# The opening of a three-block transformer kernel: shift and scale of the first norm in another order

## What is computed

```python
mod = cond @ w_mod[l] + b_mod[l]            # cond = silu(c), one row of 1024
sh1, sc1, g1, ... = jnp.split(mod, 9, axis=-1)
h = rms_norm(x, norm_g[l, 0]) * (1.0 + sc1) + sh1
x = x + 0.5 * g1 * swiglu(h, w_ffn1_gu[l], w_ffn1_down[l])
```

## Time and profile before

| | us |
|---|---|
| median of 3 runs | 1767.01 (1766.74 to 1767.05) |
| the profiled execution's own time | 1766.84 |
| its span in the trace | 1765.0 |
| PE busy in the span | 1738.3 (98%) |
| VectorE busy | 1404.0 (80%) |
| ScalarE busy | 990.8 (56%) |

### The profile page before, as it was taken

How to read it: one execution, slowest core, us unless ns; L and a number is a source line. 1 busy time by engine, 2 the same in 40 slices (tenths; PEclk the granted TensorE clock), 3 DMA queues, 4 the chain that set the end, 5 groups by cost and what they waited for, 6 DMA issues and landing times.

```text
span 1765.0 us, 25083 instructions
## 1 busy us (share of the span) xinstructions
PE 1738.3 (98%) x9402; PEld 1469.9 (83%) x9402; DVE 1404.0 (80%) x2146; ACT 990.8 (56%) x1631; POOL 184.8 (10%) x382
## 2 busy tenths in 40 slices
PE   6999999999999999999999999999999999999997
PEld 3888888888888888888888888888888888888886
DVE  6998987898899889768888866479898875688565
ACT  4443576855575556777555744556455644465444
POOL 3111012111111111021111000001110000010000
PEclk9999999999999999999999999999999999999999
DMA  9999732699869986417998554449886484466551
GB/s 342 368 345 394 279 134 81 250 344 326 319 224 340 335 310 218 168 49 299 332 333 300 213 206 158 174 184 329 323 329 254 163 303 149 183 222 251 203 195 68
DMA packets 125144, 441.12 MB, mean 250 GB/s; under 512 B 15248, under 2 KB 18144, under 8 KB 124896
## 3 DMA queue, kind: packets, MB, share of 16 engines
q1 hardware_dynamic: 91024, 315.98, 49.1%
q0 software_dynamic: 33296, 120.12, 18.0%
q10 hardware_dynamic: 704, 3.42, 0.5%
HBM read 438.38 MB, written 1.09 MB: 249 GB/s over the span
## 4 chain that ended last, share of the span: by engine, by line
PE 96%; DMA 2%; DVE 1%; SPq 0%; ACT 0%; issue 0%; DVEq 0%
PE banks L2291 21%; PE banks L2093 15%; PE banks L2071 14%; PE banks L2296 11%; PE banks L2098 8%; PE banks L2076 7%; PE banks L2241 2%; PE banks L2245 2%; PE banks L2250 2%; PE banks L2061 2%; PE banks L2063 2%; PE banks L2062 2%; DMA weights_raw<-in_w_mod_first 1%; PE banks L2207 1%; PE banks L2518 1%; PE banks L2546 1%
## 5 line engine op out<-in xcount | busy, mean ns | idle before, releaser
L1295 DVE TENSOR_TENSOR weights_lo<-weights_raw,weights_hi 128x1024 fp32r<-128x1024 f32 (+2 forms) x584 | 684.1, 1200 | 71.8 <-ACT weights_hi L775 70.9
L775 ACT ACTIVATE weights_hi<-weights_raw 128x1024 fp32r<-128x1024 f32 (+2 forms) x584 | 582.4, 1036 | 70.2 <-PE banks L2098 21.9
L2291 PE MATMUL banks<-hT,weights_hi 128*128 128x512 f32 x1600 | 400.1, 392 | 0.0
L2291 PEld LDWEIGHTS banks<-hT,weights_hi 128*128 128x128 f32 x1600 | 290.8, 189 | 54.3
L2071 PE MATMUL banks<-weights_hi,hT 128*128 128x512 f32 (+2 forms) x1152 | 282.8, 387 | 0.0
L1308 DVE CUSTOM_DVE_ANT_0 arena<-arena,mod_acc,vectors 128x1024 f32<-128x1024 f32 x216 | 267.0, 1279 | 0.0
L2071 PEld LDWEIGHTS banks<-weights_hi,hT 128*128 128x128 f32 x1152 | 212.9, 188 | 39.8 <-DVE arena L1607 0.3
L2296 PEld LDWEIGHTS banks<-hT,weights_lo 128*128 128x128 f32 x1600 | 218.3, 190 | 15.6
L966 ACT ACTIVATE arena<-banks 128x512 f32<-128x512 f32 x100 | 60.0, 600 | 303.6 <-PE banks L2296 303.3
L2296 PE MATMUL banks<-hT,weights_lo 128*128 128x256 f32 x1600 | 223.1, 282 | 0.0
L1618 DVE TENSOR_TENSOR arena<-banks,arena 128x512 f32<-128x512 f32 x100 | 68.8, 688 | 108.5 <-ACT arena L966 108.5
(11 more groups left out here) (353 smaller groups left out, 1974.6 us busy)
## 6 DMA issues: line engine op xcount, KB each, us to landing
weights_raw<-in_w_ffn_gu SPq DMA_DIRECT2D x176, 512.0 KB, 4.6
arena<-in_w_mod POOLq DMA_DIRECT2D x128, 512.0 KB, 6.1
weights_raw<-in_w_in SPq DMA_DIRECT2D x104, 512.0 KB, 4.2
weights_raw<-in_w_ffn_down SPq DMA_DIRECT2D x88, 512.0 KB, 4.9
arena<-in_w_ada POOLq DMA_DIRECT2D x88, 512.0 KB, 6.2
weights_raw<-in_w_ffn_in SPq DMA_DIRECT2D x88, 512.0 KB, 4.2
weights_raw<-in_w_ffn_out SPq DMA_DIRECT2D x44, 512.0 KB, 4.5
weights_raw<-in_w_out SPq DMA_DIRECT2D x32, 512.0 KB, 4.1
```

Source lines behind the costliest of these rows:

```text
L775: nc.scalar.activation(whi[:, n % PARTS, 0:width], raw[:, slot, 0:width], ACT.Copy).then_inc(S("hi_done"), credit(n))
L1295: V.tensor_tensor(wlo[:, n % PARTS, 0:width], raw[:, n % RING, 0:width], whi[:, n % PARTS, 0:width].bitcast(F32), ALU.subtract).then_inc(S ...
L2291: T.matmul(half_banks(j)[:, kind, :], whi[:, n % PARTS, 256 * k + P * kind:256 * k + P * (kind + 1)], hx[:, :, 4 * q + k, :], start=q == 0 ...
```

## The change

- The order of the two matrices in `w_mod_first` is swapped (done when the inputs are laid out): m = 0 to 7 are now scale, m = 8 to 15 shift. DVE stores scale's columns and computes `scale_cols` before the fourth `bias_take`.
- Of the last eight columns (shift) only the first two are extracted first (`mod_store(0, 0, 2)`); the other six follow after DVE has scaled the first half of group 0. The second half of group 0 is now scaled by ACT. PE waits for the six (`mod_stored` 3) before it writes into the second bank of the strip; ACT waits for them before its second `hi_static`.
- Weight units 6 to 9 get a semaphore each. The pairs' semaphores count one round less for slots 0 to 3.
- The window mask (384 columns, 192 KB) leaves the first load of `con` and joins the second, which grows from 768 to 960 KB. `bias_mask` waits for that load.
- PE: the fourth bias pass comes after m = 9, not 10; `x_turn(0)` after m = 8, not 9; `x_turn(1)` after m = 12, not after 15. One block of `x_turn(0)` goes to bank 1 and one to another place in bank 0.
- DVE: group 2 is scaled after `lo_static(n0)`, not before `x_low(0)`.

```diff
-BIAS_AFTER = (2, 4, 8, 10)
+BIAS_AFTER = (2, 4, 8, 9)
-X_TURN_AFTER = 9
+X_TURN_AFTER = (8, 12)
-X_BY_ACT_FIRST = (1, 4, 6, 7)
+X_BY_ACT_FIRST = (0, 1, 4, 6, 7)
...
+        def x_block(pair, k, first):
+
+            if pair == 0 and k == 1:
+                return (1, 384) if first else (5, 256)
+            if pair == 3 and k == 1 and first:
+                return 0, P
+            b, c0 = (X_AT_FIRST if first else X_AT)[pair]
+            return b, c0 + P * k
...
+        def raw_wait(eng, n):
+
+            slot = n % RING
+            if n < RING + PREFETCH:
+                home = FIRST_RING + slot
+                eng.wait_ge(S(f"first_mod_loaded{home}"), 16 * (sum(first_home(m) == home for m in range(MOD_FIRST_UNITS)) + 1))
+            else:
+                eng.wait_ge(S(f"w_loaded{slot // 2}"), 32 * (n // RING - (slot < PREFETCH)))
...
-                        sp.dma_start(raw[:, slot + u, :], w[b, 2 * h + u]).then_inc(S(f"w_loaded{slot // 2}"), 16)
+                        loaded = f"first_mod_loaded{FIRST_RING + slot + u}" if n < RING + PREFETCH else f"w_loaded{slot // 2}"
+                        sp.dma_start(raw[:, slot + u, :], w[b, 2 * h + u]).then_inc(S(loaded), 16)
...
-                        sp.dma_start(con[:, C_FIRST:], A["con"][:, C_FIRST:]).then_inc(S("const_loaded"), 16)
+                        sp.dma_start(con[:, C_MASKW:], A["con"][:, C_MASKW:]).then_inc(S("const_loaded"), 16)
...
-                act.wait_ge(S(f"w_loaded{slot // 2}"), 32 * (n // RING))
+                raw_wait(act, n)
...
-            act.dma_start(con[:, 0:C_FIRST], A["con"][:, 0:C_FIRST]).then_inc(S("const_loaded"), 16)
+            act.dma_start(con[:, 0:C_MASKW], A["con"][:, 0:C_MASKW]).then_inc(S("const_loaded"), 16)
...
                 hi_static(RING, SLOT)
                 act.wait_ge(S("scale_ready"), 1)
+                act.wait_ge(S("mod_stored"), 2)
+                x_scaled(a, 0, True, (1,))
                 x_hi(0)
                 x_scaled(a, 1, True)
                 x_hi(1)
+                act.wait_ge(S("mod_stored"), 3)
                 hi_static(RING + 1, SLOT)
...
+            def mod_store(chunk, k0=0, k1=8):
+
+                nth = 1 - chunk
+                dve.wait_ge(S("mod_summed"), nth + 1)
+                at = slice(8 * chunk + k0, 8 * chunk + k1)
+                eye = con[:, C_EYE:C_EYE + 32].unsqueeze(1).broadcast_to([P, k1 - k0, 32])
+                then(V.tensor_tensor(modm[:, k0:k1, :], bank[sum_bank(nth)][:, 32 * k0:32 * k1].rearrange("p (k j) -> p k j", j=32), eye, ALU.mult))
+                then(V.tensor_reduce(modr[:, k0:k1], modm[:, k0:k1, :], AX, ALU.add))
+                V.tensor_tensor(modc[:, at], modr[:, k0:k1], vec[:, at], ALU.add).then_inc(S("mod_stored"), 1)
...
-            mod_store(0)
+            mod_store(1)
+            scale_cols(phases[0][2])
             bias_take(3)
-            mod_store(1)
+            mod_store(0, 0, 2)
...
-                    scale_cols(a)
-                    x_scaled(a, 0, first=True)
-                    x_scaled(a, 2, first=True)
+                    dve.wait_ge(S("mod_stored"), 2)
+                    x_scaled(a, 0, (0,), first=True)
+                    mod_store(0, 2, 8)
+                    dve.wait_ge(S("mod_stored"), 3)
                     x_low(0)
                     lo_static(n0, SLOT)
+                    x_scaled(a, 2, first=True)
                     x_low(1)
...
+                            if u == 0 and t == 1:
+                                pe.wait_ge(S("mod_stored"), 3)
                             pe.wait_ge(S(sem), tr[0] + 2 * u + t + 1)
...
-                        if u == X_TURN_AFTER:
+                        if u == X_TURN_AFTER[0]:
                             pe.wait_ge(S("const_loaded"), 16)
                             x_turn(0, range(4), 1)
-                    pe.wait_ge(S("bias_taken"), len(BIAS_AFTER))
-                    x_turn(1, range(4), 1)
+                        if u == X_TURN_AFTER[1]:
+                            pe.wait_ge(S("bias_taken"), len(BIAS_AFTER))
+                            x_turn(1, range(4), 1)
                     keep_warm(WARM[0])
                     opening_strip(n0, strip_banks)
...
-    laid["w_mod_first"] = np.asarray(inputs["w_mod"])[0, :, 0:2 * D]
+    laid["w_mod_first"] = np.roll(np.asarray(inputs["w_mod"])[0, :, 0:2 * D], D, axis=1)
```

More of the change, by code:

```diff
@@ L433, in chunk_is_ready @@
             if chunk < MOD_CHUNKS[0][0]:
-                eng.wait_ge(S("mod_stored"), chunk + 1)
+                eng.wait_ge(S("mod_stored"), 1)
             elif chunk == RAW_CHUNK:
@@ L451, in x_group @@
             return hf[:, (i + g) % 4, :].rearrange("p (k n) -> p k n", k=2), (slice(2 * j, 2 * j + 2), slice(P * t, P * (t + 1)))
+        def x_block(pair, k, first):
[5 more added lines that the diff above has]
+            return b, c0 + P * k
         def x_chunk(g, i, k, first):
-            b, c0 = X_AT_FIRST[X_FIRST[g]] if first else X_AT[g]
-            if g == 0 and k == 1 and not first:
-                return hf[:, i % 4, P:2 * P], bank[5][:, 256:384]
-            return hf[:, (i + g) % 4, P * k:P * (k + 1)], bank[b][:, c0 + P * k:c0 + P * (k + 1)]
+            b, c0 = x_block(X_FIRST[g] if first else g, k, first)
+            return hf[:, (i + g) % 4, P * k:P * (k + 1)], bank[b][:, c0:c0 + P]
         def x_is_scaled(eng, k, g):
             if k == 1:
-                by = [i for i in range(X_GROUPS) if (i in X_BY_ACT_FIRST) == (g in X_BY_ACT_FIRST)]
-                eng.wait_ge(S("scaled_by_act" if g in X_BY_ACT_FIRST else "scaled_by_dve"), by.index(g) + 1)
+                if g in X_BY_ACT_FIRST:
+                    eng.wait_ge(S("scaled_by_act"), X_BY_ACT_FIRST.index(g) + 1)
+                else:
+                    eng.wait_ge(S("scaled_by_dve"), (0, 2, 3, 5).index(g) + 1)
                 return
             if g in X_BY_ACT:
-                eng.wait_ge(S("scaled_by_act"), 4 + 5 * (k - 2) + X_BY_ACT.index(g) + 1)
+                eng.wait_ge(S("scaled_by_act"), 5 * (k - 1) + X_BY_ACT.index(g) + 1)
             else:
@@ L822, in x_hi @@
                 x_is_scaled(act, o_n[0], g)
-                if g == 0 and o_n[0] > 1:
+                if g == 0:
                     act.wait_ge(S("scaled_by_dve"), 4 * (o_n[0] - 1) + 1)
@@ L1313, in raw_mod_unit @@
                 n, m = raw_unit(k), 8 * RAW_CHUNK + k
-                dve.wait_ge(S(f"w_loaded{n % RING // 2}"), 32 * (n // RING))
+                raw_wait(dve, n)
                 V.tensor_tensor_reduce(raw[:, n % RING, :], raw[:, n % RING, :], cond_row, 1.0, vec[:, m:m + 1], ALU.mult, ALU.add, modc[:, m:m + 1])\
@@ L1320, in mod_units @@
                     mod_unit(m)
-            def mod_store(chunk):
-                dve.wait_ge(S("mod_summed"), chunk + 1)
-                at = slice(8 * chunk, 8 * (chunk + 1))
-                eye = con[:, C_EYE:C_EYE + 32].unsqueeze(1).broadcast_to([P, 8, 32])
-                then(V.tensor_tensor(modm[:, :, :], bank[sum_bank(chunk)][:, 0:256].rearrange("p (k j) -> p k j", k=8), eye, ALU.mult))
-                then(V.tensor_reduce(modr[:, :], modm[:, :, :], AX, ALU.add))
-                V.tensor_tensor(modc[:, at], modr[:, :], vec[:, at], ALU.add).then_inc(S("mod_stored"), 1)
+            def mod_store(chunk, k0=0, k1=8):
[6 more added lines that the diff above has]
+                V.tensor_tensor(modc[:, at], modr[:, k0:k1], vec[:, at], ALU.add).then_inc(S("mod_stored"), 1)
             def bias_reach(q):
@@ L1351, in bias_mask @@
                 dve.wait_ge(S("bias_taken"), 6)
+                dve.wait_ge(S("const_loaded"), 32)
                 V.scalar_tensor_tensor(bias[:, :, c0:c1], bias[:, :, c0:c1], HD ** 0.5,
@@ L1417, in x_low @@
                 x_is_scaled(dve, scales[0], g)
-                if g == 0 and scales[0] > 1:
+                if g == 0:
                     dve.wait_ge(S("scaled_by_dve"), 4 * (scales[0] - 1) + 1)
@@ L1534, in scale_cols @@
             def scale_cols(a):
-                chunk_is_ready(dve, a["mod"])
+                if a["mod"] > 0:
+                    chunk_is_ready(dve, a["mod"])
                 chunk_is_ready(dve, a["mod"] + 1)
@@ L2201, in x_turn @@
                         pe.wait_ge(S("xn1b_ready"), k)
-                    b, c0 = (X_AT_FIRST if k == 1 else X_AT)[4 * t + j]
                     for i in range(2):
                         c = 2 * j + i
-                        if k > 1 and t == 0 and c == 1:
-                            b, c0 = 5, P
-                        ins = T.transpose(bank[b][:, c0 + P * i:c0 + P * (i + 1)], xn[:, t, P * c:P * (c + 1)], ident)
+                        b, c0 = x_block(4 * t + j, i, k == 1)
+                        ins = T.transpose(bank[b][:, c0:c0 + P], xn[:, t, P * c:P * (c + 1)], ident)
                     ins.then_inc(S("tr_ready"), 1)
```

## The result

The changed kernel takes 1769.80 us in the median of 20 runs (1767.09 to 1771.59), the kernel before 1767.03 in 20 runs beside it (one of them at 3523.08, which does not move the median). The ratio is 1.0015, with a 95% interval of 1.0009 to 1.0021: slower by some 2.8 us, which is within 0.2% but above the range that the prediction gave (1765.6 to 1768.4). The profiled execution took 1770.75 us with a span of 1768.9, against 1766.84 and 1765.0 before, so the two profiles differ by 3.9 us.

The account below looks back on a forecast made before the run. The down rows' start at 60.33 was taken as bound by two strings ending together, SP's loads and the strip on DVE and ACT. Only T's -0.06, rounded to -0.1, counted: from 1767.01 to 1766.9 us, range 1765.6 to 1768.4.

Parts of the forecast that it names:

- PE's list up to T: PE's opening work in its new order: PE alone would be done with m = 15 at 31.2 us.
- T: End of PE's work on modulation unit m = 15: 31.26 us before, forecast 31.2, a move of -0.06.
- that the profile ascribes to nothing: PE's 0.82 us stall in the opening, which the forecast allowed may come at m = 10.
- m = 15: Last modulation unit: its load was forecast to be issued at 25.1 and land at 30.5, bounded by 30.1 and 32.0.
- The mask's bytes: 192 KB moved into the second constants load: counted at 0; as a rival, units 10 and 11 wait, +0.48 us, 1767.4.
- DVE's list leads without a hole: From ACT's conversion of unit 10 at 43.71, DVE's list runs to 60.3, when PE starts the down rows.
- A drop of the clock in the strip, or a wait of PE behind 60 us: Signs in the profile after that would mean a cause the prediction did not have.
- the early first matmul: PE's first matmul of the strip: forecast at about 32.9 in place of 34.65, 1.75 us earlier.
- SP's string: T, constants, gains, weight units 10 and 11: nothing shortened, 12.4 us from T to the landing at 43.68.
- the 0.36 that the prediction gave DVE: The rest of the strip follows DVE and runs 0.36 us plus T's shift earlier.
- The carried early start: Rival: up to the whole 1.75 us of PE's earlier first matmul reaches 60.33, giving 1765.3; chance 0.15.
- The late last unit: Rival: `x_turn(0)` ahead of m = 9 delays m = 15's issue and landing, T + 1.4 us, 1768.4; chance 0.25.

Follow-up runs that it names:

- e3: The changed kernel with PE's list of before (bias passes after m = 2, 4, 8, 10, transposes after m = 9 and 15): 1767.47 us.
- f2: The kernel before with only the window mask moved into the second constants load: 1767.61 us.
- e1: The changed kernel with SP issuing weight units 10 and 11 ahead of the second constants load and the gains: 1767.64 us.
- h1: The kernel before with PE's new order alone (fourth bias pass after m = 9, transposes after m = 8 and 12): 1768.83 us.
- e2: The changed kernel with the window mask back in the first constants load: 1768.73 us.
- e4: The changed kernel with 24 tiny matmuls (48 instructions) more behind PE's warming ones: 1767.50 us.
- i1: The changed kernel again, unchanged, for a second profile: 1772.12 us in one run.
- g1: The kernel before with one small matmul (two instructions) more behind PE's warming ones: 1767.22 us.
- g4: The changed kernel with PE's list of before, units 10 and 11 ahead of constants and gains, and one warm matmul less: 1766.66 us.
- f1: The kernel before with SP issuing weight units 10 and 11 ahead of constants and gains: 1767.35 us.
- i2: The kernel before with only the mask moved to the second constants load, again, for a second profile: 1770.59 us in one run.

## Why the prediction was wrong

**The step that failed is "PE's list up to T".** It moved T by -0.06; in the profile after T moved by +0.60. It took the stall "that the profile ascribes to nothing" for a price of 0.82 that is paid once, wherever PE then is. In fact the stall is a date: it ends when the piece of program is there, at 27.93 before and 27.92 after. PE came to the edge 1.2 us earlier and so stood for 2.00, and its lead was gone. What counts is the work behind the edge. With the old order it is three matmuls of the bias pass and units 11 to 15: from the stall's end to T it is 2.79 in e3 (27.27 to 30.06) and 2.48 in f2 (27.91 to 30.39). With the new one three matmuls of m = 10 and `x_turn(1)` stand there in place of the bias pass's three: 3.94 after (27.92 to 31.86), 3.95 in e1, 3.94 in h1. That is some 1.3 us over e3 and f2, and 0.6 over the kernel before itself, where m = 15 came last, with a wait of 0.64, and the same stretch was 3.33. The order alone costs 1.6 us in the median (h1). To this comes a price that the prediction didn't have: in e2, e4 and i1 PE is still at 1.2 GHz behind the stall (granted clock 0.50), a group of 19 takes 2.77 us instead of 1.49, and T slides to 32.9 to 35.4. The prediction's 31.2 was 0.7 off in the profile after and up to 4 off in such an execution. PE alone set T, not the last unit: in each of these m = 14 and m = 15 run as one group of 16.

**m = 15.** Forecast to be issued at 25.1 and to land at 30.5; it was issued at 24.4 and landed 5.6 later, at 30.0. The row chosen for it, 5.4, was the right one. The Trainium skill's figures ("DMA: Bandwidth & Descriptors", the section on the anatomy of one DMA) made an estimated 3.2 us; the trace's 5.6 does not agree with that. The section is on loads that GpSimd issues, and this one was issued by SyncE, so the estimate was taken from a case that is not this one.

**The mask's bytes.** Taken as 0 with 0.48 as the bound. From T to ACT's unit 10 it was 12.45 us before and 13.24 after. Over the ten profiles with the mask later and SP's old order it is 11.80 to 13.54, 12.73 in the mean; over the four with the mask in its old place (before, g1, h1, e2) 11.83 to 12.76, 12.37 in the mean. The difference of 0.4 is near the price of the bytes, but smaller than the spread of either group, so no price is shown. In f2 T came sooner, as forecast (30.39), and the median was still 1767.61, against 1767.21 beside it. The DMA engines do run dry between the issue of unit 11 and its landing (8 GB/s at some 37.8 us before), but whether that covers the bytes isn't shown: in the profile after this transfer took 0.65 longer than before.

**The rest of the path to 60.33.** "DVE's list leads without a hole" made the down rows follow unit 10. That holds only while PE keeps up with it: a late DVE made PE wait, a piece of its program then came late, and the clock fell. 1.4 us of lateness became 4.0. In the profile after this is the larger part: DVE's last bias result, at 61.7, would have let the down rows start 1.4 late, and the other 2.6 us are the stall and the clock, which the prediction had at nothing. The stall and its packet go together in every profile; that the wait made the packet late is argued and not shown. The prediction named "A drop of the clock in the strip, or a wait of PE behind 60 us" as causes that it didn't have; the wait, the stall and the drop came between 52 and 64 us, behind the strip.

**What held.** The change stayed within the 0.2% that a measurement can tell, as forecast with 0.94. T to `x_scaled` 0.77 (forecast 0.80); 0.22 for 64 elements and 0.35 for 192 (0.23 and 0.38); unit 7's low part at T + 5.16 (T + 5.44); unit 6 no longer waiting for 7 and converted from 31.28 (some 31). By the Trainium skill ("VectorE: DVE Perf Modes", the section on the fixed extra latency) the estimate for 64 elements was 0.19; the trace has 0.22, a little above. That the early first matmul is not carried to the end is right. ACT waited 1.34 us for unit 10 with SP's string as it was. With that string out of the way (e1) PE's first matmul comes 1.5 us earlier behind T than before, and the down rows 0.31 (28.76 against 29.07): near the 0.36 that the prediction gave DVE.

**The rivals.** The carried early start was worked out at 1.75 us; with SP's string out of the way it gives 0.3 at the down rows in e1, and in g4, the best version, nothing: its 1.0 is T's. The late last unit was on the right side, with the wrong mechanism: m = 15 landed 0.6 us earlier than before, not later. In the profile after, T's share came from PE's own list and the larger share from the second stall and the clock.

## What to carry to other kernels

A stall marked "issue" inside an unbroken group of small matmuls is not a price but a date: look for the packets of the instruction queue, and count the work that stands behind the edge up to the step that others wait for, since work moved ahead of it gains nothing and work moved behind it delays that step. Where two strings end together, shortening one of them gains nothing (f1). And where single executions spread over more than the effect, profile the same kernel twice before naming a cause: the first profile of f2 showed only its good side.

## What the runs showed of the hardware that was not expected

- Instructions come through a DMA queue of their own in packets of 16.4 KB (75 of them, 1.23 MB), while the data queues move about 400 GB/s. A bias pass of 64 matmuls, 128 instructions with the weight loads, runs in 0.64 us; where the next piece isn't there, PE stands until 2.5 to 3.0 us after the start of the half-microsecond slice that has the packet: 0.6 to 2.7 us in the 21 stalls followed here.
- The load of a piece is early in some executions and late in others of the same kernel (f2 at 49 to 51 us, i2, the same kernel, at 55 to 57).
- After a stall of 1.5 to 1.9 us the granted clock was 0.56 for the next 3.7 us in one profile, and the same eight matmuls took 3.5 to 3.7 us in three; in e3, behind a stall of 2.16, they took 2.11, the full speed.
